# Expert feed-forward in a two-layer block: where the down weights are split, in what order the third tile is asked for, and which operand of the last router products stands still

## The reference, cut to what matters

```python
x = x + jnp.einsum('bse,ed->bsd', mix, w_out[layer])
h2 = rmsnorm(x, norm2_w[layer])
# hier_moe(h2, ...):
p_group  = jax.nn.softmax(x32 @ wg + bg, axis=-1)            # 4 groups
e_logits = (x32 @ we + be).reshape(t, 4, 8)                  # 32 experts
...                                                          # top group, then top 2 experts in it
order = jnp.argsort(ids); xs = xf[order // TOP_K]            # 2048 rows, sorted by expert
hg = lax.ragged_dot(xs, w_gate, sizes)                       # 1024 -> 512
hu = lax.ragged_dot(xs, w_up, sizes)                         # 1024 -> 512
ys = lax.ragged_dot(jax.nn.silu(hg) * hu, w_down, sizes)     # 512 -> 1024
```

## Time and profile before

| | us |
|---|---|
| three runs | 4133.52, 4139.14, 4139.69 |
| median of them | 4139.14 |
| the profiled execution | 4142.12 |
| its span in the profile | 4140.3 |
| PE busy | 3631.0 (88%) |
| DVE busy | 2830.5 (68%) |
| last router products begin, in the span | 1146.71 |
| expert stage, from its first transfer to the next stage's | 1157.87 to 1809.17 |

### The profile page before, as it was taken

How to read it: one execution, slowest core, us unless ns; L and a number is a source line. 1 busy time by engine, 2 the same in 40 slices (tenths; PEclk the granted TensorE clock), 3 DMA queues, 4 the chain that set the end, 5 groups by cost and what they waited for, 6 DMA issues and landing times. The chain is left out here.

```text
span 4140.3 us, 62371 instructions
## 1 busy us (share of the span) xinstructions
PE 3631.0 (88%) x24735; PEld 2927.8 (71%) x24735; DVE 2830.5 (68%) x3464; ACT 1609.6 (39%) x2136; POOL 72.4 (2%) x56
## 2 busy tenths in 40 slices
PE   6999996879959999948999776649999897999897
PEld 4888885767848888836888432319997676888786
DVE  4775325977559999978886588685555557667356
ACT  3222212545537777754333120253333133322244
POOL 0000000000020000010000000000000000000000
PEclk8999998999969999978999888779999998999999
DMA  5942225536579999953332331340111332222565
GB/s 199 337 166 92 88 76 194 192 112 214 181 278 420 413 411 411 399 194 102 102 122 102 124 123 69 117 166 26 42 34 63 102 117 77 82 91 73 187 192 170
DMA packets 262498, 689.49 MB, mean 167 GB/s; under 512 B 30136, under 2 KB 126072, under 8 KB 235754
## 3 DMA queue, kind: packets, MB, share of 16 engines
q1 hardware_dynamic: 226474, 559.75, 37.8%
q10 hardware_dynamic: 20528, 67.11, 4.3%
q0 software_dynamic: 15248, 59.14, 3.9%
HBM read 530.81 MB, written 172.96 MB: 170 GB/s over the span
## 5 line engine op out<-in xcount | busy, mean ns | idle before, releaser
L157 PE MATMUL g_ps<-h1T_hi,g_w_lo 128*128 128x512 f32 x448 | 175.4, 392 | 6.9 <-DVE g_w_lo L356 6.9
L1775 DVE TENSOR_TENSOR moe_wg_lo<-moe_wg,moe_wg_hi 128x2048 fp32r<-128x2048 f32 x68 | 153.1, 2288 | 35.6 <-ACT moe_wg_hi L1629 35.5
L159 PE MATMUL g_ps<-h1T_hi,g_w_hi 128*128 128x512 f32 x448 | 174.8, 390 | 0.0
L158 PE MATMUL g_ps<-h1T_lo,g_w_hi 128*128 128x512 f32 x448 | 174.8, 390 | 0.0
L4164 DVE TENSOR_TENSOR x3T_lo<-fd_w_raw,x3T_hi 128x1024 fp32r<-128x1024 f32 x66 | 80.8, 1224 | 122.6 <-ACT x3T_hi L4093 122.4
L1775 DVE TENSOR_TENSOR moe_wu_lo<-moe_wu,moe_wu_hi 128x2048 fp32r<-128x2048 f32 x68 | 152.9, 2288 | 16.3 <-ACT moe_wu_hi L1629 16.3
L1775 DVE TENSOR_TENSOR moe_wd_lo<-moe_wd,moe_wd_hi 128x2048 fp32r<-128x2048 f32 x66 | 148.3, 2289 | 14.9 <-ACT moe_wd_hi L1629 14.9
L2882 PE MATMUL rs_banks<-rs_pm,rs_qx 64*64 64x64 f32 x2048 | 157.2, 217 | 0.0
L157 PE MATMUL fd_acc<-x3T_hi,x3T_lo 128*128 128x512 f32 x352 | 139.2, 395 | 19.9 <-DVE x3T_lo L4167 19.9
L157 PE MATMUL g_ps<-x2T_hi,g_w_lo 128*128 128x512 f32 x352 | 139.8, 397 | 17.1 <-DVE g_w_lo L583 17.1
L157 PE MATMUL g_ps<-g_w_hi,h1T_lo 128*128 128x512 f32 x384 | 149.6, 390 | 0.0
(11 more groups left out here) (738 smaller groups left out, 10776.4 us busy)
## 6 DMA issues: line engine op xcount, KB each, us to landing
moe_wg<-in_exp_w_gate SPq DMA_DIRECT2D x68, 1024.0 KB
moe_wu<-in_exp_w_up SPq DMA_DIRECT2D x68, 1024.0 KB
moe_wd<-in_exp_w_down SPq DMA_DIRECT2D x66, 1024.0 KB
fd_w_raw<-in_ffn_w_down SPq DMA_DIRECT2D x66, 512.0 KB, 4.5
go_w_raw<-in_w_out SPq DMA_DIRECT2D x64, 512.0 KB, 4.4
g_w<-in_w_in SPq DMA_DIRECT2D x52, 512.0 KB, 4.8
g_w<-in_w_in SPq DMA_DIRECT2D x22, 1024.0 KB, 7.7
s_xs<-g_zero POOLq DMA_DIRECT2D x2, 8192.0 KB, 34.3
```

The source lines that it names most:

```text
L157: pe.matmul(out, l[1], r[0], start=(k == 0), stop=False)
L158: pe.matmul(out, l[0], r[1], start=False, stop=False)
L159: return pe.matmul(out, l[0], r[0], start=False, stop=(k == kt - 1))
L1775: v.tensor_tensor(lo[:, q * m:q * m + m], w[:, q * m:q * m + m], hi[:, q * m:q * m + m], ALU.subtract).then_inc(sem_lo, 1)
```

## The change

1. **Router.** For the last two tiles the operands are swapped: stationary the 36 columns of `f`, moving the 128 columns of `t`, into `acc[0:36]`. ACT copies the 36 x 128 result to `pair`, PE turns it into `go_pl`, and DVE copies the logits as before.
2. **Down weights.** ACT's `high(d_in, ...)` and DVE's `low(d_hi, ...)` of a tile move from the end of its step to the head of the next. The waits for the weights' landing stay at the end of ACT's step.
3. **Scatter.** `moved` becomes two semaphores, one for the first 8 scatters and one for the last 8. ACT waits for the first ahead of `wd_hi`, DVE for the second ahead of `wd_lo`, SP for both ahead of the rows of tile 2.
4. **Third tile.** SP's step 1 is unrolled. In it gate and up weights of tile 2 are asked for first; then comes the wait for the scatter, the rows of tile 2, and the down weights of tile 1.

```diff
+            def rows_x(j, b, n_used):
+                sp.dma_start(x[:, 1 - b], xs.rearrange("(j p) n -> j p n", p=P)[j + 1],
+                             cond=(n_used > j + 1)).then_inc(x_in[1 - b], 16)
...
-                if not first:
+                if not isinstance(j, int):
                     sp.wait_ge(turned, past(j))
-                    sp.dma_start(x[:, 1 - b], xs.rearrange("(j p) n -> j p n", p=P)[j + 1],
-                                 cond=(n_used > j + 1)).then_inc(x_in[1 - b], 16)
+                    rows_x(j, b, n_used)
                 for q in range(2):
                     sp.wait_ge(g_lo, past(j * 2 + (q + 1)))
                     weights(g_in, wg, w_gate, e1, j + 1, new1, q)
                 for q in range(2):
                     sp.wait_ge(u_lo, past(j * 2 + (q + 1)))
                     weights(u_in, wu, w_up, e1, j + 1, new1, q)
+                if isinstance(j, int) and j == 1:
+                    sp.wait_ge(turned, past(j))
+                    for m in moved:
+                        sp.wait_ge(m, 16 * NT)
+                    rows_x(j, b, n_used)
...
-                if isinstance(j, int) and j == 0:
-                    sp.wait_ge(moved, 16 * 2 * NT)
-            steps(sp, 1, step)
+            steps(sp, 2, step)
...  ACT, step
+                if not first:
+                    act.wait_ge(moved[0], 16 * NT)
+                    high(d_in, d_hi, wd, wd_hi, j * 16)
                 act.wait_ge(gated, past(j + 1))
...
+                for q in range(2):
+                    act.wait_ge(d_in[q], past(j * 16 + 16))
                 if first:
-                    act.wait_ge(moved, 16 * 2 * NT)
-                high(d_in, d_hi, wd, wd_hi, j * 16 + 16)
+                    act.nop()
...  DVE, step
                 if not first:
+                    v.wait_ge(moved[1], 16 * NT)
+                    low(d_hi, d_lo, wd, wd_hi, wd_lo, j)
                     v.wait_ge(at_hi, past(j))
...
-                low(d_hi, d_lo, wd, wd_hi, wd_lo, j + 1)
...  deep_norm, PE, after the last pass
-                for t in passes[-1]:
-                    rate(t)
+                for i, t in enumerate(passes[-1]):
+                    pe.wait_ge(by_dve, past(t + 1))
+                    for k in range(ND):
+                        mm = products3(pe, acc[0:nf, t % n_acc, 0:P], [h[:, k] for h in (f_hi, f_lo)],
+                                       [h[:, t % 2, k] for h in (t_hi, t_lo)], k, ND)
+                    mm.then_inc(pair_done, 1)
+                for i, t in enumerate(passes[-1]):
+                    pe.wait_ge(pair_ok, past(i + 1))
+                    mm = pe.transpose(pl[:, t, 0:nf], pair[0:nf, t % 2], ident[0:nf, 0:nf])
+                mm.then_inc(rated, 1)
...  ACT, after the last pass
+                for i, t in enumerate(g):
+                    act.wait_ge(pair_done, past(i + 1))
+                    act.activation(pair[0:nf, t % 2], acc[0:nf, t % n_acc, 0:P], ACT.Copy).then_inc(pair_ok, 1)
```

More of the change, by code:

```diff
@@ L1471, in moe @@
         w_in = [s.sem(f"w_in{n}") for n in "gud"]
-        moved = s.sem("moved", soft=True)
+        moved = [s.sem(f"moved{n}", soft=True) for n in range(2)]
         x_first = [s.sem(f"x_first{j}", soft=True) for j in range(NA)]
@@ L1813, in _ @@
                     pool.indirect_dma_start(xs[:, :], bass.IndirectOffsetOnAxis(ap=slots[:, k, t:t + 1], axis=0),
-                                            h2_rows[:, t], None).then_inc(moved, 16)
+                                            h2_rows[:, t], None).then_inc(moved[t // (NT // 2)], 16)
 def combine_norm(nc, ys, gate2, slots, x, w, ident, hT, x14, x2, y_out, tap_src, par, w_two, w_src):
@@ L3932, in deep_norm @@
             pt, pl = s.ps("pt", [P, ND, P]), s.ps("pl", [P, NT, 64])
-            f_high, f_low, turned, by_act, by_dve, rated = (s.sem(n) for n in (
-                "f_high", "f_low", "turned", "by_act", "by_dve", "rated"))
+            f_high, f_low, turned, by_act, by_dve, rated, pair_done, pair_ok = (s.sem(n) for n in (
+                "f_high", "f_low", "turned", "by_act", "by_dve", "rated", "pair_done", "pair_ok"))
+            pair = s.sb("pair", [P, 2, P])
             few_in = s.sem("few_in", soft=True)
@@ L4241, in _ @@
                     low(t)
-                v.wait_ge(rated, past(NT))
+                v.wait_ge(rated, past(NT - 1))
                 v.tensor_copy(logits[:, :, :], pl[:, :, 0:nf])
```

## The result

The changed kernel takes 4177.3 us (median of 3 runs, 4175.9 to 4179.0) against 4139.1: 1.009 times, with a 95% interval from 1.0075 to 1.0105. It is slower by 38 us. The prediction was 4134, with a range from 4124 to 4142, and its chance for "slower by more than 0.2%" was 0.07.

What follows compares the result with a forecast made beforehand. PE, never idle in the expert stage's body (530.00 of 530.00 us), was taken as the bound, so only the ends could move. -3.9 + 0.9 - 2.1 = -5.1 from 4139.1 gave 4134.0, range 4124 to 4142.

Steps and rivals of the forecast that it cites:

- part 3: Expert stage, down-weight splits moved across the step boundary: nothing in the body, -2.1 us at the stage's end.
- Part 1: Last router products with swapped operands: 0.107 us apart, logits' copy starts earlier, -3.9 us.
- the bound of -4.9: Router products: largest gain allowed, if PE's clock rises in the dense products of tile 7.
- Part 2: Third tile's early weight loads: 10.0 us lost ahead of the scatter's end, 9.1 gained behind it, +0.9 us.
- slow short stream: Rival, router: products of 128 moving columns run at the two-pass rate, 0.44 us cold; +10.7 us in all, 4149.8; chance 0.10.
- Free early loads: Rival, third tile: early weight loads don't hold the scatter up, so all 9.1 us are gained; -15.1, 4124.0; chance 0.12.
- the clock rises: Rival, router and scatter: PE's clock rises and the scatter's thin tail is filled; -8.0 us, 4131.1; chance 0.18.
- The two rivals on the slower side: Router products at the two-pass rate, +10.7 us, chance 0.10; scatter held up far more, +8 and more, chance 0.03.
- if PE showed a wait in the body: Expert stage's body: one of three listed signs that would make the prediction wrong; no size given.

Runs made afterwards that it cites:

- experiment 3: On the kernel of experiment 1, ACT's store of `y` goes ahead of its splits, each half waiting only for its own landing: 4163.58 us, ratio 1.0067.
- experiment 4: The kernel before with one edit, ACT's store of `y` ahead of its splits of the down weights: 4170.43 us, ratio 1.0074.
- experiment 5: On the kernel of experiment 3, both landing waits ahead of the store; only the changed kernel's boundary between store and splits is missing: 4162.95 us, ratio 1.0057.
- experiment 7: The kernel before with the router's operand swap alone: 4136.44 us, ratio 0.9995.
- experiment 1: The changed kernel with ACT's down-weight splits back at the end of the step, ahead of the store of `y`: 4131.44 us, ratio 0.9983.
- experiment 2: On the kernel of experiment 1, ACT waits for both landed halves ahead of the first split, store still behind: 4133.62 us, ratio 0.9991.
- experiment 8: The kernel of experiment 1 with fewer third-tile weight loads ahead of the scatter's end: two 4126.4 us (again 4125.5), one 4124.6, none 4130.1.

## Why the prediction was wrong

The step that failed is in part 3: "In the body the order of DVE is the same, so nothing. ACT's store of `y` goes ahead of the splits; nobody waits for it." Nobody waits for the store, but the store waits: for DVE's copy of `y`. What stands behind it on ACT, the splits of `wd`, is what DVE waits for next. The term that was put at nothing measured +41.5 us. The premise under it, that the edits keep each engine's order of work in the body, was wrong too: ACT's store and splits changed places.

Most of its price could be read before. DVE had 485.56 of 530.00, 16.4 a step of 17.91, so 1.5 of slack. The circle is the copy's end to the store's issue 0.24, the store 0.34, the boundary 0.4 (0.7 in the other body), and the first half of `wd_hi` 1.9: 2.9 to 3.2 in which DVE does nothing. Less the slack of 1.5 that is about 1.5 a step; 1.39 were lost. (In the changed kernel DVE has 16.2 of work and 3.07 of this wait a step, which nearly make up the 19.30.) Of the 41.5 us the order of store and splits brings 26 to 27 (experiments 3 to 5: 563.3 to 564.9 against 537.4), the step boundary between them 14 to 16.

- **Part 1, -3.9: right in kind, too small.** -5.5 came. The shape was as forecast, 0.107 between products in tile 6 (1146.51, 1146.61, 1146.72), but the granted clock rose from the 0.50 level to 1.00 at the end of tile 6, near 1148.6, after PE had worked without a gap since 1144.55, and the 24 products of tile 7 took 1.4 in place of 2.5; that is beyond the bound of -4.9, which had left some of them cold and had kept the tail of 1.2 at the cold rate (0.87 came). The slow short stream did not show.
- **Part 2, +0.9: right.** The scatter's end moved 9.8 (10.0 forecast), `p_a` came 17.1 after it (17.7), and the sum is +0.1 where +0.9 stood. One pair of traces can't tell such a difference: from the stage's start to `p_a` the three traces with the order of before have 89.4, 88.0 and 91.1 (experiments 4 and 7), the six with four loads ahead 89.5 to 91.3, and the means, 89.5 and 90.5, are 1.0 apart. Over 1190 to 1199 q1 and q0 moved 347 and 345 packets and 2.58 and 1.24 MB in the changed kernel, like the earlier trace rows at two thirds. The Trainium skill, "DMA: Bandwidth & Descriptors", section "Queues, rings and completion order", has the engines take turns packet by packet; the trace agrees. PE stood 14.88 ahead of `p_x` and DVE 17.90 ahead of `wd_lo`, 13 and 17 forecast.
- **Part 3, -2.1 at the end: right where it can be seen.** In experiments 1, 2 and 8 the last `p_a` is 22.3 from the next stage's first transfer, and 24.47 before. In the changed kernel it is 25.69, ACT last (1845.7) and DVE 4.8 ahead of it, since ACT's last store waits for a DVE that is late (copy of `y` 1837.93, store 1838.86).
- **Rivals.** Free early loads fell (the scatter moved). That the clock rises held. The two rivals on the slower side were about the router's products and the scatter; none was about a wait inside the body, though "if PE showed a wait in the body" stood under what would make the prediction wrong. It did: 0.4 a step for `aT_lo` and 0.5 for `xT_lo`.

With ACT's splits ahead of its store again (experiment 1) the kernel took 4131.4, where the sum of the parts gave 4134: the forecast of the two ends was sound, and the miss is the body alone.

## What to carry to other kernels

Before an instruction is moved ahead of others on an engine, list what it waits for, not only who waits for it: if that comes from an engine which itself waits for what now stands behind, a circle is closed, and its length is added to that engine's work in every step. Compare it with that engine's slack a step. Where the DMA engines are full, asking early for weights holds up a bulk transfer on another queue by about the weights' own time (four loads of 1 MB cost the scatter 9.8 to 10.5 us here, and 4.19 MB at 0.418 MB/us are 10.0); ask ahead only for as much as its consumers can't get in time otherwise.

## What the runs showed of the hardware

The DMA engines' busy share did not tell whether they were the limit. From 1300 to 1700, before (first row) and changed (second), by queue q1:

```profile
q1 hardware_dynamic: 22558, 152.70, 93.8%
...
```

```profile
q1 hardware_dynamic: 20868, 140.94, 92.7%
```

A packet took 0.938 x 16 x 400 / 22558 = 0.266 us before and 0.284 after, at the same size: with fewer bytes asked for, the packets lengthened until the share was the same, though the transfers set nothing there (experiment 1 brings back 410 GB/s with the loads where they are). The Trainium skill, "Perfetto Trace Analysis", section "Identifying the Most-Contended Engine", calls the occupancy of the DMA engines misleading, because there are 16 of them, and takes the utilization of the memory (HBM) in its place; these rows agree that the share misleads and that the bytes moved tell more.

For products of 128 moving columns with 36 stationary ones, in the type of three products to one, PE needs 0.107 at the 0.50 clock and about 0.06 at full clock (24 from 1148.87 to 1150.27), where 128 stationary and 36 moving columns took 0.213 at the 0.50 clock.

PE's granted clock did not follow from its being busy alone. Before, PE was busy without a gap from 1146.70 to 1157.10 and stayed at the 0.50 level (1.2 GHz) all that time; with the swapped operands it reached the 1.00 level (2.4 GHz) near 1148.6, about 4 us after its last wait had ended. After the wait for the third tile's rows it stayed at 0.50 for 3 to 6 us of work, in kernels with the same program at that place. Which property of the stream makes the difference, these runs don't separate.
